# Order of the query products and one attention pipeline per layer in a three-layer transformer kernel

## The chip, the cores and the metric

The kernel runs on one core of a Trainium2 chip. The metric is the device time of one execution in microseconds (us). Everything is fp32. TensorE (PE) does matmuls and transposes, VectorE (DVE) and ScalarE (ACT) the elementwise work, SyncE (SP) issues the loads of the weights.

## The reference, cut to what matters

Three layers over 512 latent rows (x), the first two of them also with 256 context rows (c). Each layer has two attention branches, a and b, whose q, k and v are products of the same normalised input h:

```
p = h @ w_in[l]                          # 1024 wide; k, v, q of both branches, convolution, gates
ka, kb, qa, qb = rope(rmsnorm(head) * gain)   # per head of 64
o_a = softmax(qa ka' / 8) va             # layers 0, 1: all keys, latent and context
o_b = softmax(qb kb' / 8, sink) vb       # layers 0, 1: a window of 128 each way, and the context
o_c = short_conv(p)
x = x + gt1 * ((g_a*(o_a@w0) + g_b*(o_b@w1) + g_c*(o_c@w2)) @ w_out)
x = x + gt2 * expert_choice_ffn(...)     # layers 0 and 1 only
```

Layer 0 also computes the context rows' outputs. Layer 1 needs only keys and values of the context. Layer 2 has a branch a with a causal band and a branch b with a dilated causal pattern, gates of its own, and no experts.

## The kernel before, in words

Activations lie transposed, features on the partitions and rows along the free axis. A product of 128 output features takes 8 pairs of weight load and matmul for 512 columns, and in the layers with context columns 8 more for the 256; 128 features of weights are half of a 1 MB chunk, and the chunks come through a ring of six buffers that SP fills in the order of use (L1014): a chunk is loaded as soon as the last product of the chunk six before it is through.

The order of work is a list of jobs written out by hand for each layer (`plan_layer` L296, `plan_second` L314). Every engine goes through the same list and does its part of each job, in that order:

- `("qk", l, name)`: the product of a q or k (TensorE), its square into `sq` (ACT), the copy of the product into its buffer (DVE). The copy releases the PSUM slot.
- `("hs", ...)`: one matmul that sums the squares by head, the square root into `rs` (ACT), `reciprocal` (L1434) and the scaling (L1436) (DVE).
- `("rot", ...)`: one matmul that permutes for the rotation (L762), three DVE operations (L1440 to L1443).
- `("v", l, n)`: 96 matmuls of 128 columns (L727) and a copy by ACT.
- `pipelined` (L278) puts behind each job of a list the `rot` of the qk two before it and the `hs` of the qk before it.

A PSUM slot of two banks is taken for every product, `hs`, `rot` and `v`, three slots in turn (L629 `begin`), so in a row of qk jobs each product gets the slot of the product before it. ACT's square of a job waits until the `hs` before it has read `sq` (L1188), and the root of an `hs` waits until the rotation before it is through with `rs`.

Attention is worked on in units: one tile of 128 queries times a pair of heads. `attention_order` (L247) makes a software pipeline over the units of one branch, a step per unit s: S(s) are its scores (L773, into slots 0 and 1; the step waits for both), E(s) the masked copy with row maximum (DVE L1510) and the exponential (ACT L1132), T(s-1) the transposes (L785) and their copies, V the product with v for two units (L818), spread over two steps and three steps late; Q, K, R and O are the row sums and the scaled output of four units (one tile). A pipeline of n units has n+3 steps. Layer 0 has 24 units per branch (the last eight are context units with 2 tiles of keys), layers 1 and 2 have 16. Units of branch a have 6 tiles of keys in layers 0 and 1, units of b 4 or 5; in layer 2 they have 1 or 2 (a) and 1 to 4 (b).

Before, layers 0 and 1 go: ka, va, kb, vb, qa0 to qa3, the pipeline of branch a, qb0 to qb3, the pipeline of branch b, convolution, gates. Both branches' queries lie in the same buffer `qbuf` (`q3`), so qb can't be made ahead of the end of branch a. Layer 2 makes all k, q and v and its gates first (`plan_second`), and then goes through two pipelines one after the other.

```
            first = [("qk", l, "ka"), ("v", l, 0), ("qk", l, "kb"), ("v", l, 1)]
            first += [("qk", l, f"qa{j}") for j in range(4)]
...
            order = pipelined(first) + attention_order((l, 0))
            order += pipelined([("qk", l, f"qb{j}") for j in range(4)])
            order += attention_order((l, 1)) + conv + gates[2] + gates[0] + gates[1]
```

Of the kernel before, what the change touches and what calls it, by code (L numbers as in the profile page):

```python
# [101 lines left out]
def program(nc, x, c, ctx_in, c_ctx, w_ada, b_ada, g_mix, g_ffn, w_in, qg_a, kg_a, qg_b, kg_b, sink_b, conv_w,  # L102
            w_branch, w_out, w_router, w_e_gate, w_e_up, w_e_down, norm_gain_2, w_in_2, q_norm_a_2, k_norm_a_2,
            sinks_a_2, q_norm_b_2, k_norm_b_2, w_out_2, consts, out):
    with ExitStack() as stack:
# [104 lines left out]
        def units_first(l, br):  # L210
            units = []
            streams = [("x", i) for i in range(NX // P)] + ([("c", i) for i in range(NC // P)] if l == 0 else [])
            for st, i in streams:
                q0, mask = (i * P if st == "x" else NX + i * P), None
                if st == "c":
                    segs, lo, hi, tiles = [(0, NC, NX)], 0, NC, [4, 5]
                elif br == 0:
                    segs, lo, hi, tiles = [(0, NX, 0), (NX, NC, NX)], 0, NT, list(range(6))
                elif i == 0:
                    segs, lo, hi, tiles, mask = [(512, 2 * P, 0), (768, NC, NX)], 512, 1024, [0, 1, 4, 5], 3 * P  # L220
                else:
                    n = min(3, NX // P + 1 - i)
                    segs, lo, hi, mask = [(256, NC, NX), (512, n * P, (i - 1) * P)], 256, 512 + n * P, 0
                    tiles = [4, 5] + [i - 1 + m for m in range(n)]
                for g in range(4):
                    units.append(dict(q0=q0, t=q0 // P, g=g, heads=(g, 4 + g), kj=br,
                                      segs=segs, lo=lo, hi=hi, tiles=tiles, mask=mask, vcols=(0, HD)))
            return units

        def units_second(br):  # L230
            units = []
            for i in range(NX // P):
                a = max(0, i - 1) if br == 0 else 0
                n = (i - a + 1) * P
                for g in range(4):
                    heads = (g, 4 + g) if br == 0 else (2 * g, 2 * g + 1)
                    units.append(dict(q0=i * P, t=i, g=g, heads=heads, kj=0 if br == 0 else g, segs=[(0, n, a * P)],
                                      lo=0, hi=n, tiles=list(range(a, i + 1)),
                                      mask=M_BAND + 2 * P - n if br == 0 else M_DIL + 4 * P - n,
                                      vcols=(0, HD) if br == 0 else (P + heads[0] * HD, P + heads[1] * HD)))  # L240
# [6 lines left out]
        def attention_order(key):  # L247

            units = UNITS[key]
            n = len(units)  # L250
            order = []
            for s in range(n + 3):
                banks = (len(units[s - 1]["tiles"]) + 1) // 2 if 1 <= s <= n else 0
                if s < n:
                    order.append(("S", key, s))
                if s % 4 == 0 and 4 <= s <= n:
                    order.append(("Q", key, s // 4 - 1))
                if banks:
                    order.append(("T", key, s - 1, 0))
                if s < n:  # L260
                    order.append(("E", key, s))
                    if s % 4 == 3 and key in SINK:
                        order.append(("K", key, s // 4))
                if banks > 1:
                    order.append(("T", key, s - 1, 1))
                if s % 4 == 1 and s >= 5:
                    order.append(("R", key, s // 4 - 1))
                if s >= 3:
                    h, part = (s - 3) // 2, (s - 3) % 2
                    if h < n // 2:  # L270
                        order.append(("V", key, h, part))
                        if part and h % 2:
                            order.append(("O", key, h // 2))
                if banks > 2:
                    order.append(("T", key, s - 1, 2))
            return order
# [311 lines left out]
        def last_rot(key):  # L588
            return ("rot", key[0], "qb3" if key[1] else "qa3")
# [12 lines left out]
        def turned_to(j):  # L602

            key, p, b = j[1:]
            n = min(2, len(UNITS[key][p]["tiles"]) - 2 * b)
            to = turned[key[0] == 2][:, p // 2 % 2, 2 * b:2 * b + n, :, p % 2, :]
# [3 lines left out]
        def last_v(key):  # L610
            return ("v", key[0], 2 if key == (2, 1) else key[1])
# [6 lines left out]
        def _(pe):  # L618
# [76 lines left out]
            def run(j):  # L695
                kind, l = j[0], j[1]
                if kind in ("qk", "conv_c", "conv_x", "conv_b", "gate", "silg", "branch", "wout"):
# [4 lines left out]
                    if kind == "branch":  # L702
# [3 lines left out]
                        elif d == 0:  # L706
                            need(oT_ready, ("O", (l, br), len(UNITS[l, br]) // 4 - 1))
                        product(j, None, w, q3 if br == 2 else o4[:, br], wd, 4)
                    elif kind == "wout":
                        if j[2] == 0 and l < 2:  # L710
                            need(gate_used, ("branch", l, 1, KD - 1))
                        elif j[2] == 0:
                            need(oT_ready, ("O", (2, 0), NX // P - 1))
                            need(oT_ready, ("O", (2, 1), NX // P - 1))
# [49 lines left out]
                elif kind == "S":  # L764
                    u = UNITS[j[1]][j[2]]
                    q, k, _ = attn_bufs(j[1])
                    if j[2] == 0:
                        need(q_ready, last_rot(j[1]))
# [24 lines left out]
                elif kind == "V":  # L793
                    key, h, late = j[1:]
                    u = UNITS[key][2 * h]
                    v = attn_bufs(key)[2]
                    if h == 0 and not late:
                        need(v_ready, last_v(key))
                    n = o_number[key, h // 2]
                    if not late:  # L800
                        for r in range(2):
                            last = [t for t in bank_jobs[r] if t[0] == "T" and t[1] == key and t[2] // 2 == h]
# [5 lines left out]
                    exps = turned[key[0] == 2][:, h % 2]  # L808
                    tiles, own = u["tiles"], key == (2, 1)
                    steps = [(g, m, a) for g in (range(2) if own else (None,)) for m in range(len(tiles)) for a in range(2)]  # L810
                    cut = len(steps) // 4 * 2 or 1
                    for g, m, a in steps[cut:] if late else steps[:cut]:
                        r = slice(a * HD, (a + 1) * HD)
                        if own:
                            out_, exp_, col = ps[r, b + g * P:b + (g + 1) * P], exps[:, m, a, g, :], UNITS[key][2 * h + g]["vcols"][a]
# [311 lines left out]
        def _(act):  # L1127
# [46 lines left out]
            def run(j):  # L1174
# [64 lines left out]
                elif kind == "R" and j[1][0] < 2:  # L1239
# [118 lines left out]
        def _(dve):  # L1358
# [63 lines left out]
            def run(j):  # L1422
                kind, l = j[0], j[1]
                w = width(l, j[2] if kind in ("qk", "hs") else "") if kind not in ("S", "E", "K", "Q", "T", "R", "V", "O") else 0
# [71 lines left out]
                elif kind == "S":  # L1496
# [5 lines left out]
                    for a in range(2):  # L1502
# [6 lines left out]
                        least = nsink[:, SINK[j[1]], h:h + 1] if j[1] in SINK else 3.0e38  # L1509
# [3 lines left out]
                    if j[2] % 4 == 3 and j[1] in SINK:  # L1513
                        sink = by_pair(sinks[:, SINK[j[1]], :])
                        V.do(v.tensor_tensor(sinkd[:, t % 2, :].rearrange("p (g a) -> p g a", a=2), sink,
                                             nms[:, t % 2, :].rearrange("p (g a) -> p g a", a=2), ALU.add), sd_ready, ("K", j[1], t))
                elif kind == "Q":
                    key, t = j[1:]
                    V.need(p_ready, ("E", key, 4 * t + 3, 1))
                    if key in SINK:  # L1520
                        V.need(sx_ready, ("K", key, t))
                        V.do(v.tensor_tensor(lsum[:, t % 2, :], lsum[:, t % 2, :], sinke[:, t % 2, :], ALU.add))
                    V.do(v.reciprocal(rden[:, :], lsum[:, t % 2, :]))
                    if t > 0:
                        V.need(tb_full[bank_of["R", key, t - 1]], ("R", key, t - 1))
# [8 lines left out]
                elif kind == "R" and j[1][0] == 2:  # L1534
                    r = bank_of[j]
                    sg = sg2[:, 4 * j[1][1]:4 * j[1][1] + 4, j[2] * P:(j[2] + 1) * P]
# [3 lines left out]
                elif kind == "O":  # L1540
                    (l, br), t = j[1:]
                    V.need(pv_done, ("V", j[1], 2 * t + 1, 1))
# [3 lines left out]
                    if l < 2:  # L1546
                        V.need(tb_done[bank_of["R", j[1], t]], ("R", j[1], t))
# [155 lines left out]
```

How the kernel before makes its waits and increments, by code:

```python
            def meet():  # L623
                phases[0] += 1
                pe.sem_inc(s_phase, 1)
                pe.wait_ge(s_phase, 4 * phases[0])
# [1 line left out]
            def begin(key, slot=None):  # L629
                if slot is None:
                    slot, turn[0] = turn[0], (turn[0] + 1) % 3
                if slot == 2 and in_banks[0]:
                    for r in range(2):
                        pe.wait_ge(tb_done[r].sem, bank_at[r])
                    in_banks[0] = False
                n = used[slot]
                used[slot] += 1
                job[key] = [slot, n, None]
                if n:
                    pe.wait_ge(free[slot], n)
                return BANK[slot]
# [8 lines left out]
            def begin_bank(j):  # L651
                r = bank_of[j]
                if not in_banks[0]:
                    pe.wait_ge(free[2], used[2])
                    in_banks[0] = True
                if bank_at[r]:
                    pe.wait_ge(tb_done[r].sem, bank_at[r])
                bank_at[r] += 1
                return TBANK[r]
# [1 line left out]
            def weights(key):  # L662
                n = chunk_key[key]
                slot, value = chunk_at[n]
                pe.wait_ge(w_full[slot], value)
                return n, slot
# [1 line left out]
            def need(ev, key):  # L669
                pe.wait_ge(ev.sem, ev.at[key])
# [24 lines left out]
            def run(j):  # L695
# [36 lines left out]
                    if j == FIRST[0]:
                        pe.wait_ge(sil_ready, 1)
                    b = begin(j)
```

## Time and profile before

| | us |
|---|---|
| median of 3 runs | 3743.57 (3741.46 to 3747.7) |
| the profiled execution | 3751.16 |
| its span, first to last instruction | 3749.4 |
| TensorE busy | 3290.6 (88%) |
| VectorE busy | 886.3 (24%) |
| ScalarE busy | 622.7 (17%) |
| TensorE clock granted, mean | 0.951 |

The span is one execution, and all rows below are from it. TensorE's end times are modelled, so a matmul's busy time runs some 0.16 us into the next group; where a duration matters it is read from start to start. "Idle before" in a timeline is the time in which the engine had nothing to do ahead of a group, and the arrow names what ended it. "DVEq L1117" is VectorE's release of a PSUM slot.

### The profile page before, as it was taken

Reading aid. Unit: us, or ns where it says so; the run is one execution under the profiler, and the core shown is the slowest. Engines: PE = TensorE matmul, PEld = TensorE weight load, DVE = VectorE, ACT = ScalarE, POOL = GpSimd, SP = SyncE. Lnnn points to the kernel's source line nnn. Section 1 sums busy time; section 2 is a strip of 40 time slices with the busy share of each in tenths; the row PEclk is TensorE's granted clock in tenths of the full one; section 3 lists DMA queues with packets and bytes.
Section 4 is the critical chain, followed back from the end, with each engine's and each line's share of the span. In section 5 each row is a group of like instructions: output and inputs, shape, how many; then the busy total and the mean of one; then the engine's idle time right before and its main releaser. Section 6 shows DMA issues by size and latency. Waiting matters only on the chain. (4 is left out here: it accounts for less than half of the span.)

```text
span 3749.4 us, 36326 instructions
## 1 busy us (share of the span) xinstructions
PE 3290.6 (88%) x14258; PEld 1628.0 (43%) x14258; DVE 886.3 (24%) x1357; ACT 622.7 (17%) x1072; POOL 16.8 (0%) x35
## 2 busy tenths in 40 slices
PE   5887899989995999999987979999778788778978
PEld 3544555545554442433344544444423223233544
DVE  2464611001114001111024562011300010025342
ACT  2162600000002100101021541000201001011141
POOL 1000000000000000000000000000000000000000
PEclk8989999999996999999988989999799999999989
DMA  7100012353510778697851001232188998961200
GB/s 205 45 1 23 1 45 79 124 174 106 169 56 12 262 277 313 238 347 255 313 151 45 1 23 57 58 88 79 34 317 298 356 329 312 358 200 45 68 1 23
DMA packets 381924, 551.94 MB, mean 147 GB/s; under 512 B 65496, under 2 KB 177384, under 8 KB 381640
## 3 DMA queue, kind: packets, MB, share of 16 engines
q1 hardware_dynamic: 379856, 546.53, 42.8%
q0 software_dynamic: 1600, 3.20, 0.3%
q8 instruction: 107, 1.75, 0.2%
q14 instruction: 49, 0.40, 0.0%
q10 hardware_dynamic: 312, 0.05, 0.0%
HBM read 547.63 MB, written 2.10 MB: 147 GB/s over the span
## 5 line engine op out<-in xcount | busy, mean ns | idle before, releaser
L692 PE MATMUL ps<-hT,ring 128*128 128x512 f32 (+1 forms) x2576 | 973.9, 536 | 72.8 <-ACT hT L1132 28.4
L899 PE MATMUL ps<-ring,hT 128*64 128x512 f32 x3072 | 716.8, 604 | 112.3 <-DMA ring<-in_w_e_up 41.2
L692 PEld LDWEIGHTS ps<-hT,ring 128*128 128x128 f32 x2576 | 492.5, 192 | 545.1 <-issue 492.1
L899 PEld LDWEIGHTS ps<-ring,hT 128*64 128x64 f32 x3072 | 202.0, 137 | 604.4 <-issue 401.7
L692 PE MATMUL ps<-obuf,ring 128*128 128x512 f32 (+1 forms) x512 | 198.5, 540 | 2.5 <-DMA ring<-in_w_branch 1.5
L1659 DVE SCALAR_TENSOR_TENSOR xT<-ps,mod,xT 128x512 f32<-128x512 f32 x96 | 63.5, 662 | 535.1 <-PE ps L967 281.1
L905 PE MATMUL ps<-ring,hT 128*32 128x512 f32 x1536 | 184.7, 598 | 0.0
L1132 ACT ACTIVATE prob<-prob,nms 128x768 f32<-128x768 f32 (+5 forms) x224 | 159.2, 711 | 59.9 <-DVE nms L1510 51.8
L1132 ACT ACTIVATE prob<-ps 128x512 f32<-128x512 f32 (+1 forms) x56 | 38.6, 689 | 733.0 <-PE ps L692 733.0
L862 PE MATMUL ps<-obuf,merged 128*128 128x256 f32 x640 | 153.3, 389 | 7.3 <-DVE obuf L1611 4.1
L785 PE MATMUL ps<-con,prob 128*128 128x128 f32 x872 | 135.8, 291 | 26.4 <-ACT prob L1132 25.2
L773 PE MATMUL ps<-kbuf,qbuf 64*128 64x256 f32 (+3 forms) x640 | 124.2, 502 | 26.4 <-DVEq L1117 16.7
L1434 DVE RECIPROCAL rs<-rs 128x512 f32<-128x512 f32 (+1 forms) x33 | 129.9, 3935 | 72.8 <-ACT rs L1132 72.4
L692 PE MATMUL ps<-merged,ring 128*128 128x512 f32 (+1 forms) x384 | 139.7, 526 | 4.1 <-issue 4.1
L692 PEld LDWEIGHTS ps<-obuf,ring 128*128 128x128 f32 x512 | 96.2, 190 | 99.4 <-issue 93.8
L785 PEld LDWEIGHTS ps<-con,prob 128*128 128x128 f32 x872 | 96.8, 146 | 92.3 <-ACT prob L1132 52.0
L862 PEld LDWEIGHTS ps<-obuf,merged 128*128 128x128 f32 x640 | 119.9, 195 | 35.2 <-issue 20.7
L963 PE MATMUL ps<-kbuf,obuf 128*128 128x512 f32 x256 | 115.7, 592 | 0.0
L1475 DVE TENSOR_TENSOR prob<-prob,ps 128x768 f32<-128x768 f32 (+1 forms) x32 | 26.3, 822 | 358.0 <-PE ps L692 358.0
L1643 DVE TENSOR_TENSOR qbuf<-qbuf,ps 128x1536 f32<-128x1536 f32 (+1 forms) x16 | 23.8, 1488 | 340.8 <-ACT qbuf L1132 340.8
L692 PEld LDWEIGHTS ps<-merged,ring 128*128 128x128 f32 x384 | 73.4, 192 | 70.4 <-issue 67.1
L1645 DVE TENSOR_TENSOR qbuf<-qbuf,ps 128x1536 f32<-128x1536 f32 (+1 forms) x16 | 23.8, 1488 | 317.4 <-PE ps L905 162.4
(185 smaller groups left out, 2292.3 us busy)
## 6 DMA issues: line engine op xcount, KB each, us to landing
ring<-in_w_e_gate SPq DMA_DIRECT2D x256, 512.0 KB, 7.4
ring<-in_w_e_up SPq DMA_DIRECT2D x256, 512.0 KB, 8.2
ring<-in_w_e_down SPq DMA_DIRECT2D x256, 512.0 KB, 7.8
ring<-in_w_in SPq DMA_DIRECT2D x49, 1024.0 KB, 5.2
ring<-in_w_ada SPq DMA_DIRECT2D x48, 1024.0 KB, 11.6
ring<-in_w_in SPq DMA_DIRECT2D x48, 256.0 KB, 5.0
ring<-in_w_branch SPq DMA_DIRECT2D x16, 512.0 KB, 7.3
ring<-in_w_out SPq DMA_DIRECT2D x8, 1024.0 KB, 8.6
```

The source lines that it names most:

```text
L692: mm = pe.matmul(ps[:, b + a:b + e], lhs[:, k, :], rhs[:, k, a:e], start=k == 0, stop=k == nk - 1)
L773: mm = pe.matmul(ps[:, b[a] + c0:b[a] + c0 + w], q[r, u["g"], u["q0"]:u["q0"] + P], k[r, u["kj"], k0:k0 + w], start=True, stop=True)
L785: mm = pe.transpose(ps[:, o:o + P], scored(j[2], a, u)[:, m * P:(m + 1) * P], ident)
L862: mm = pe.matmul(ps[:, o:o + 2 * P], tok[:, t, d * P:(d + 1) * P], selx[:, t, :], start=t == 0, stop=t == 3)
L899: mm = pe.matmul(ps[e * CX:(e + 1) * CX, b + pair * 512:b + (pair + 1) * 512], lhs[:, k, s0:s0 + CX], expert_dst(slot, e)[:, k % 2, :], st ...
L905: mm = pe.matmul(ps[e * CC:(e + 1) * CC, b + 1024:b + 1536], lhs[:, k, s0:s0 + CC], expert_dst(slots[e // 2], e % 2)[:, k % 2, :], start=k ...
L963: mm = pe.matmul(ps[:, o:o + NX], ye[:, g, d * P:(d + 1) * P], gTx[:, g, :], start=g == 0, stop=g == 1)
L1132: return sc.activation(o, i, f, **kw)
L1434: V.do(v.reciprocal(rs[:, 0:w], rs[:, 0:w]))
L1475: V.do(v.tensor_tensor(g, g, ps[:, b:b + w], ALU.mult))
L1643: step(v.tensor_tensor(g, g, banks(("eg", half)), ALU.mult))
L1659: step(v.scalar_tensor_tensor(xT[:, d, a:e], ps[:, o:o + e - a], mod3[:, l, GT2 + d, a // 512:a // 512 + 1], xT[:, d, a:e], ALU.mult, ALU. ...
```

## The change

In layers 0 and 1 the queries of branch a and b go into `obuf` (`o4`), each into the place where its branch's output will lie: scores of tile t read queries of tile t, and the output of tile t is written after them. So all eight query products come before attention. The two v products are moved from behind ka and kb to the end of the list. In all three layers the units of both branches form one list and one pipeline (48+3 steps in layer 0, 32+3 in layers 1 and 2, in the place of two times 24+3 and 16+3). Waits that a branch's first unit had (rotated queries, values ready) are kept for the first unit of each branch. Job names lose the branch; `Q`, `O`, `R` and `K` are numbered through both branches. No arithmetic, no load and no matmul is added or taken away.

```
-        UNITS = {(l, br): units_first(l, br) for l in range(DEPTH) for br in range(2)}
-        UNITS |= {(2, br): units_second(br) for br in range(2)}
+        UNITS = {l: units_first(l, 0) + units_first(l, 1) for l in range(DEPTH)}
+        UNITS[2] = units_second(0) + units_second(1)
+        TILES = {l: len(UNITS[l]) // 8 for l in UNITS}
...
         def plan_layer(l):
-            first = [("qk", l, "ka"), ("v", l, 0), ("qk", l, "kb"), ("v", l, 1)]
-            first += [("qk", l, f"qa{j}") for j in range(4)]
+            first = [("qk", l, "ka"), ("qk", l, "kb")] + [("qk", l, f"{w}{j}") for w in ("qa", "qb") for j in range(4)]
+            first += [("v", l, 0), ("v", l, 1)]
...
-            order = pipelined(first) + attention_order((l, 0))
-            order += pipelined([("qk", l, f"qb{j}") for j in range(4)])
-            order += attention_order((l, 1)) + conv + gates[2] + gates[0] + gates[1]
+            order = pipelined(first) + attention_order(l) + conv + gates[2] + gates[0] + gates[1]
...
-            return (pipelined(first) + attention_order((2, 0)) + attention_order((2, 1))
-                    + [("wout", 2, d) for d in range(KD)])
+            return pipelined(first) + attention_order(2) + [("wout", 2, d) for d in range(KD)]
...
         def qk_dest(l, name):
             if l < 2:
-                return {"ka": k3[:, 0, :], "kb": k3[:, 1, :]}.get(name) if name[0] == "k" else q3[:, int(name[2]), :]
+                return {"ka": k3[:, 0, :], "kb": k3[:, 1, :]}.get(name) if name[0] == "k" else o4[:, "ab".index(name[1]), int(name[2]), :]
...
-        def attn_bufs(key):
-            l, br = key
+        def attn_bufs(l, br):
             if l < 2:
-                return q3, k3, lambda t, c0: v4[:, br, t, c0:c0 + HD]
+                return o4[:, br], k3, lambda t, c0: v4[:, br, t, c0:c0 + HD]
...
+        def first_of_branch(l, p):
+            return p % (len(UNITS[l]) // 2) == 0
...
                 elif kind == "S":
-                    if j[2] == 0:
-                        need(q_ready, last_rot(j[1]))
+                    if first_of_branch(l, j[2]):
+                        need(q_ready, last_rot(l, u["br"]))
...
                 elif kind == "V":
-                    if h == 0 and not late:
-                        need(v_ready, last_v(key))
+                    if first_of_branch(l, 2 * h) and not late:
+                        need(v_ready, last_v(l, u["br"]))
```

## Rows read from the trace of the kernel before

**Rows 1.** The page: busy time and share of the span by engine.
```profile
PE 3290.6 (88%) x14258; PEld 1628.0 (43%) x14258; DVE 886.3 (24%) x1357; ACT 622.7 (17%) x1072; POOL 16.8 (0%) x35
```
**Rows 2.** Stretches: us, busy PE, PEld, DVE, ACT, POOL, then clock, DMA share, GB/s.
```profile
87.16:200.54 113.38, 90.04 (x390) 59.24 (x388) 54.03 (x36) 13.15 (x15) 0.00 (x0) 0.91 0.11 38
303.60:381.01 77.41, 54.08 (x154) 29.54 (x152) 36.71 (x25) 9.41 (x10) 0.00 (x0) 0.84 0.09 27
1965.47:2059.36 93.89, 74.61 (x317) 45.10 (x315) 45.50 (x36) 11.44 (x15) 0.00 (x0) 0.91 0.14 45
2143.89:2201.61 57.72, 38.66 (x82) 15.40 (x80) 28.18 (x25) 7.71 (x10) 0.00 (x0) 0.84 0.11 37
```
**Rows 3.** Timeline of TensorE, layer 0, ahead of branch a's attention.
```profile
99.17 10.48 PE L692 MATMUL ps<-hT,ring 128*128 128x512 f32 x32
109.49 1.02 PE L762 MATMUL ps<-kbuf,con 128*128 128x512 f32 x2
110.35 10.88 PE L727 MATMUL ps<-ring,hT 128*128 128x128 f32 x96
...
145.14 10.48 PE L692 MATMUL ps<-hT,ring 128*128 128x512 f32 x32
...
156.32 1.45 PE L756 MATMUL ps<-sq,con 128*128 128x512 f32 x4
159.98 10.56 PE L692 MATMUL ps<-hT,ring 128*128 128x512 f32 x32 [2.21 <-DVEq L1117]
...
184.24 2.08 PE L762 MATMUL ps<-qbuf,con 128*128 128x512 f32 x2 [11.56 <-DVE qbuf L1436]
...
196.04 2.08 PE L762 MATMUL ps<-qbuf,con 128*128 128x512 f32 x2 [7.16 <-DVE qbuf L1436]
200.54 2.93 PE L773 MATMUL ps<-kbuf,qbuf 64*128 64x512 f32 x8 [2.42 <-DVE qbuf L1443]
```
**Rows 4.** Timeline of ScalarE, layer 0, ahead of branch a's attention.
```profile
189.98 1.28 ACT L1132 ACT_TABLE_LOAD   x1
```
**Rows 5.** Stretches: DMA behind layer 0's first product; layer 2's row of qk jobs.
```profile
76.00:97.00 21.00, 20.20 (x119) 15.25 (x118) 5.74 (x9) 6.87 (x11) 0.00 (x0) 0.98 0.00 0
...
3394.00:3494.00 100.00, 81.84 (x181) 32.72 (x180) 62.15 (x55) 12.16 (x19) 0.00 (x0) 1.00 0.20 48
```
**Rows 6.** Timeline of TensorE, layer 2, two of its qk jobs.
```profile
3406.75 7.11 PE L692 MATMUL ps<-hT,ring 128*128 128x512 f32 x16 [1.73 <-DVEq L1117]
3414.02 1.13 PE L762 MATMUL ps<-qbuf,con 128*128 128x512 f32 x2 [0.17 <-DVE qbuf L1436]
...
3417.73 7.11 PE L692 MATMUL ps<-hT,ring 128*128 128x512 f32 x16 [1.73 <-DVEq L1117]
```
**Rows 7.** Timeline of VectorE, layer 2, in one of these jobs.
```profile
3409.83 3.35 DVE L1434 RECIPROCAL rs<-rs 128x512 f32<-128x512 f32 x1 [0.88 <-ACT rs L1132]
```
**Rows 8.** Stretches: ends and beginnings of the attention pipelines, columns as in rows 2.
```profile
299.40:303.60 4.20, 2.75 (x22) 1.52 (x20) 0.63 (x2) 2.47 (x7) 0.00 (x0) 1.00 0.00 0
381.01:393.24 12.23, 9.12 (x40) 6.20 (x41) 5.30 (x14) 5.20 (x12) 0.00 (x0) 0.59 0.00 0
393.24:471.88 78.64, 71.48 (x497) 42.82 (x497) 49.28 (x128) 54.03 (x129) 0.00 (x0) 0.96 0.01 1
2136.70:2143.89 7.19, 6.45 (x53) 4.10 (x52) 1.48 (x4) 2.72 (x6) 0.00 (x0) 1.00 0.01 2
2201.61:2213.20 11.59, 8.52 (x40) 5.88 (x41) 5.30 (x14) 4.96 (x11) 0.00 (x0) 0.62 0.00 0
3624.70:3634.00 9.30, 5.11 (x36) 2.88 (x37) 3.97 (x17) 4.51 (x17) 0.00 (x0) 0.98 0.00 0
```
**Rows 9.** Timeline of VectorE, first scores of branch a in layer 0.
```profile
208.87 0.96 DVE L1510 CUSTOM_DVE_ANT_0 prob<-ps,zero 128x768 f32<-128x768 f32 x1 [3.14 <-PE ps L773]
...
212.97 0.96 DVE L1510 CUSTOM_DVE_ANT_0 prob<-ps,zero 128x768 f32<-128x768 f32 x1 [1.14 <-PE ps L773]
```
**Rows 10.** Stretches of low or full clock, columns as in rows 2.
```profile
216.00:288.00 72.00, 70.88 (x506) 42.88 (x503) 42.90 (x91) 51.13 (x101) 0.00 (x0) 1.00 0.00 1
...
3582.00:3598.00 16.00, 11.92 (x44) 6.16 (x42) 6.39 (x29) 9.46 (x30) 0.00 (x0) 0.51 0.01 2
```

More of the change, by code:

```diff
@@ L225, in units_first @@
                 for g in range(4):
-                    units.append(dict(q0=q0, t=q0 // P, g=g, heads=(g, 4 + g), kj=br,
+                    units.append(dict(br=br, q0=q0, t=q0 // P, g=g, heads=(g, 4 + g), kj=br,
                                       segs=segs, lo=lo, hi=hi, tiles=tiles, mask=mask, vcols=(0, HD)))
@@ L236, in units_second @@
                     heads = (g, 4 + g) if br == 0 else (2 * g, 2 * g + 1)
-                    units.append(dict(q0=i * P, t=i, g=g, heads=heads, kj=0 if br == 0 else g, segs=[(0, n, a * P)],
+                    units.append(dict(br=br, q0=i * P, t=i, g=g, heads=heads, kj=0 if br == 0 else g, segs=[(0, n, a * P)],
                                       lo=0, hi=n, tiles=list(range(a, i + 1)),
@@ L254, in attention_order @@
                 if s < n:
-                    order.append(("S", key, s))
+                    order.append(("S", l, s))
                 if s % 4 == 0 and 4 <= s <= n:
-                    order.append(("Q", key, s // 4 - 1))
+                    order.append(("Q", l, s // 4 - 1))
                 if banks:
-                    order.append(("T", key, s - 1, 0))
+                    order.append(("T", l, s - 1, 0))
                 if s < n:
-                    order.append(("E", key, s))
-                    if s % 4 == 3 and key in SINK:
-                        order.append(("K", key, s // 4))
+                    order.append(("E", l, s))
+                    if s % 4 == 3 and (l, units[s]["br"]) in SINK:
+                        order.append(("K", l, s // 4))
                 if banks > 1:
-                    order.append(("T", key, s - 1, 1))
+                    order.append(("T", l, s - 1, 1))
                 if s % 4 == 1 and s >= 5:
-                    order.append(("R", key, s // 4 - 1))
+                    order.append(("R", l, s // 4 - 1))
                 if s >= 3:
@@ L270, in attention_order @@
                     if h < n // 2:
-                        order.append(("V", key, h, part))
+                        order.append(("V", l, h, part))
                         if part and h % 2:
-                            order.append(("O", key, h // 2))
+                            order.append(("O", l, h // 2))
                 if banks > 2:
-                    order.append(("T", key, s - 1, 2))
+                    order.append(("T", l, s - 1, 2))
             return order
@@ L586, in program, with last_rot @@
         PARAM_DMAS = (3 + 1 + 8 + 1 + 2, 3 + 1 + 8 + 1 + 1 + 8 + 1)
-        def last_rot(key):
-            return ("rot", key[0], "qb3" if key[1] else "qa3")
+        def last_rot(l, br):
+            return ("rot", l, "qb3" if br else "qa3")
         def scored(p, a, u):
@@ L602, in turned_to, with last_v @@
         def turned_to(j):
-            key, p, b = j[1:]
-            n = min(2, len(UNITS[key][p]["tiles"]) - 2 * b)
-            to = turned[key[0] == 2][:, p // 2 % 2, 2 * b:2 * b + n, :, p % 2, :]
+            l, p, b = j[1:]
+            n = min(2, len(UNITS[l][p]["tiles"]) - 2 * b)
+            to = turned[l == 2][:, p // 2 % 2, 2 * b:2 * b + n, :, p % 2, :]
             at = TBANK[bank_of[j]]
             return to, ps[:, at:at + n * 256].rearrange("p (k a t) -> p k a t", k=n, a=2)
-        def last_v(key):
-            return ("v", key[0], 2 if key == (2, 1) else key[1])
+        def last_v(l, br):
+            return ("v", l, 2 if (l, br) == (2, 1) else br)
+        def first_of_branch(l, p):
+            return p % (len(UNITS[l]) // 2) == 0
         o_number = {j[1:]: n for n, j in enumerate(of("O"))}
@@ L793, in run @@
                 elif kind == "V":
-                    key, h, late = j[1:]
-                    u = UNITS[key][2 * h]
-                    v = attn_bufs(key)[2]
-                    if h == 0 and not late:
-                        need(v_ready, last_v(key))
-                    n = o_number[key, h // 2]
+                    h, late = j[2:]
+                    u = UNITS[l][2 * h]
+                    v = attn_bufs(l, u["br"])[2]
+                    if first_of_branch(l, 2 * h) and not late:
+                        need(v_ready, last_v(l, u["br"]))
+                    n = o_number[l, h // 2]
                     if not late:
                         for r in range(2):
-                            last = [t for t in bank_jobs[r] if t[0] == "T" and t[1] == key and t[2] // 2 == h]
+                            last = [t for t in bank_jobs[r] if t[0] == "T" and t[1] == l and t[2] // 2 == h]
                             if last:
@@ L1238, in run @@
                     A.do(sc.copy(*turned_to(j)), tb_done[r], j)
-                elif kind == "R" and j[1][0] < 2:
+                elif kind == "R" and l < 2:
                     r = bank_of[j]
@@ L1423, in run @@
                 kind, l = j[0], j[1]
-                w = width(l, j[2] if kind in ("qk", "hs") else "") if kind not in ("S", "E", "K", "Q", "T", "R", "V", "O") else 0
+                w = width(l, j[2] if kind in ("qk", "hs") else "")
                 if kind == "adat":
@@ L1508, in run @@
                         h = u["heads"][a]
-                        least = nsink[:, SINK[j[1]], h:h + 1] if j[1] in SINK else 3.0e38
+                        least = nsink[:, SINK[l, u["br"]], h:h + 1] if (l, u["br"]) in SINK else 3.0e38
                         V.do(v.tensor_tensor_reduce(scored(j[2], a, u), ps[:, b + u["lo"]:b + u["hi"]], mask, -SCALE, least,
@@ L1512, in run @@
                         V.release(j + (a,))
-                    if j[2] % 4 == 3 and j[1] in SINK:
-                        sink = by_pair(sinks[:, SINK[j[1]], :])
+                    if j[2] % 4 == 3 and (l, u["br"]) in SINK:
+                        sink = by_pair(sinks[:, SINK[l, u["br"]], :])
                         V.do(v.tensor_tensor(sinkd[:, t % 2, :].rearrange("p (g a) -> p g a", a=2), sink,
@@ L1533, in run @@
                     V.do(v.tensor_copy(*turned_to(j)), tb_done[r], j)
-                elif kind == "R" and j[1][0] == 2:
+                elif kind == "R" and l == 2:
                     r = bank_of[j]
-                    sg = sg2[:, 4 * j[1][1]:4 * j[1][1] + 4, j[2] * P:(j[2] + 1) * P]
+                    br, t = divmod(j[2], TILES[2])
+                    sg = sg2[:, 4 * br:4 * br + 4, t * P:(t + 1) * P]
                     V.need(tb_full[r], j)
```

35 lines of the change are left out of this document (17 added, 18 removed).

## The prediction

> **What bounds the kernel now.** The page first: TensorE is busy 88% of the span, nothing else over 24% [rows 1], so what can be won without less work are the 12% in which TensorE idles or runs at the low clock. The stretches by stage come next, since the change touches only a few. In layers 0 and 1 the products ahead of branch a's attention take 113.4 and 93.9 us, the qb products ahead of branch b's 77.4 and 57.7; TensorE is busy 90.0, 74.6, 54.1 and 38.7 us of that, at a mean clock of 0.84 to 0.91 [rows 2]. The timeline shows where the holes are: not among the first products, where a v product (10.9 us) covers the chain of the job before, but behind the last one. There hs, square root, reciprocal, scaling and rotation of two jobs run out with nothing beside them: idle 11.6, 7.2 and 2.4 us, and what is left of TensorE's work runs at 1.2 GHz (the rotation takes 2.08 us in the place of 1.02) [rows 3]. This tail of some 28 us comes four times, twice in each of the layers 0 and 1. The engines beside are no bound there: VectorE is busy in half of each stretch at most [rows 2].
>
> **The sum, layer 0.** Durations from start to start [rows 3]: a product 10.32, rot 0.86, hs 1.45 less the overlap of 0.16, so 1.29, v 10.72 us. Where qk jobs follow each other, each product waits for the slot of the one before (its square and copy): a gap of some 2.4 us, and a period of 159.98 - 145.14 = 14.84 us. Before, this gap comes once in each of the two stretches, since v products or first jobs fill the other places. After, from the end of the first product: kb, hs, qa0, rot, hs = 24.1; seven periods (qa1 to qb3) = 103.9; then gap 2.4, v, rot, hs, v, rot = 26.8; and about 1.0 until the rotation's slot is free for the first scores. Together 155.8 us. The chain of the last query (root, reciprocal 5, scaling 1, some 8 us in all) fits behind the last v product of 10.7. Before it is 113.4 + 77.4 = 190.8 [rows 2]. Gain 35.0 us: four idle tails less, six or so gaps more.
>
> **Layer 1.** Queries are 512 wide, a product is 6.87 us. The nearest rows are layer 2's, whose jobs already follow each other so, 512 wide: period 3417.73 - 3406.75 = 10.98 us, with 1.7 us ahead of the product and 0.2 ahead of the rotation, which waits for VectorE's scaling [rows 6]. The period is the chain's: square, copy, three operations of the rotation, root, reciprocal 3.35, scaling, rot, hs [rows 7]. After, from the end of ka's product: kb 10.3, hs 1.3, qa0 6.9, a wait of about 1.4 for ka's scaling, rot 0.9, hs 1.3 = 22.0; one period lengthened by kb's 768 columns to about 13.0; six of 10.98 = 65.9; 1.9 to the start of v; v, rot, hs, v, rot and the slot = 25.0. Together 127.8 against 93.9 + 57.7 = 151.6 [rows 2]. Gain 23.8 us.
>
> **Where the branches join.** Three steps of running out and three of filling become three steps that do both. Layer 0: 4.2 + 12.2 us before; a step of branch b takes (78.6 - 4.2)/21 = 3.5 us on average, three 10.6 [rows 8]. Gain 5.8. Layer 1: 7.2 + 11.6 before. TensorE's work in it is 6.5 us and 8.5 at a clock of 0.62, so about 5.3 at full clock: 11.8, and with a wait or two 12.3 [rows 8]. Gain 6.5. Layer 2: 9.3 us with 5.1 of work [rows 8]; its steps wait for the exponentials anyway, so I take about half of the idle time: 2.0, between 0 and 4.2.
>
> **The first scores.** They start at 1.2 GHz now. VectorE waits 3.14 us for the scores of such a step and 1.14 at full clock [rows 9]; the two first steps of each layer could be some 1.4 us shorter, 2.8 for a layer, 5.6 for both. This asks that the clock stays up while the pipeline fills. Against it: in layer 2 the fill begins behind dense products and the clock is at 0.51, all but 1.2 GHz, through 16 us of it [rows 10]; its units are smaller than these. For it: the row of gapped jobs in layer 2 [rows 5] and steady attention [rows 10] hold 1.00. I take one of the two: 2.8, between 0 and 5.6; it can't be a loss, since these steps run at the low clock already.
>
> **What costs nothing, and its cover.** The DMAs: both k and v products use the same chunk, so the kv chunks are held until the v products at the end. All six chunks up to qb fit into the ring of six, and behind layer 0's first product there is no traffic any more [rows 5], so they have landed. What comes later is SP's load of the first two convolution chunks, which now waits for v0 and v1; the cover is the whole of attention. Were it gone, six chunks of 1 MB would come one by one. Position of the v products: their first reader is V three steps into attention, behind both copies. Queries in `obuf`: same size and engine, no operation more. In-order engines: ACT's copy of v1 stands ahead of the first exponential only, VectorE's last rotation ahead of the first row maximum; both are in the 1.0 us above. The gaps grow from one of 2.4 us per stretch to seven in a row: cover for the clock is that layer 2's ten such jobs ran at 1.00 [rows 5]. ACT's tables: one switch to the square root and one back less in each of the two layers. The load takes 1.28 us and ends 4.8 us before the rotation that TensorE waits for [rows 3, 4], while VectorE's reciprocal runs, so I count 0. "ScalarE: Activation LUTs" of the Trainium skill (section "What ACT_TABLE_LOAD costs") asks 2.66 us for every switch, drain included, and by it the sum would be up to 10.6 us larger; the trace agrees with its load time but shows it off the path here.
>
> **Sum.** 35.0 + 23.8 + 5.8 + 6.5 + 2.0 + 2.8 = 75.9 us. Against the profiled execution's 3751.2 us this gives 3675.3; that execution is 7.6 us above the median of the runs, so for the median 3743.6 - 75.9 = **3667.7, say 3668 us**.
>
> **Rivals.**
> (1) *The joined pipeline brings nothing.* The steps at the join could be as long as the old ones together, as each then holds S of branch b, T and V of a, and waits for the ACT chain; and the fill falls to the low clock. Then only the products' gain stays: 58.8, 3685 us. For it: layer 2's steps wait for ACT. Against: in layers 0 and 1 TensorE is busy in most of such steps. Chance 0.12.
> (2) *More than counted.* The fills keep the clock (2.8 more), layer 2's join gives all 4.2, and of layer 0's end, where the last steps now are as before, nothing. 3663, and with a join in layers 0 and 1 that is bounded by TensorE alone (2 to 3 us more each) 3657. Chance 0.15.
> (3) *The other side: the low clock in the gapped rows.* Place: the seven periods of qk jobs in layers 0 and 1. Price: at 1.2 GHz the 12.5 us of TensorE's work in a period of layer 0 and some 8.6 in layer 1 double: 7 x 12.5 + 7 x 8.6 = 148 us. Then 3668 + 148 = 3816, slower by 72. It decides from the point where over half of these periods run at the low clock (75.9 of 148 us). For it: the clock did fall to 1.2 GHz in the tails, with holes of 7 to 12 us [rows 2, 3]. Against it: 100 us of layer 2 with holes of 1.7 us every 11 and a clock of 1.00 [rows 5, 6]; layer 0's holes of 2.2 are longer but come at every 15 us. Chance 0.03.
> (4) *The chain of the products moves only.* If something that isn't in the trace serialises v and the last queries (a slot, `sq`), each layer keeps one tail half: 12 us less gain in each, 3692. In the slot order, products and v share one slot, rot and hs have the other two, and I find no such wait. Chance 0.04. That the change doesn't do what it says, no change of time, is about 0.01: the lists are plain.
>
> **How the numbers follow.** The forecast has 0.65, rivals 0.12, 0.15, 0.03, 0.04 and 0.01. Unknown costs around the forecast are the fills (0 to 5.6), the joins (layer 2 0 to 4.2; 2 each elsewhere), and 3 us to each side for the spread of the runs; with 3657 of rival 2 and most of 3685 of rival 1 this is 3654 to 3684. A measurement of this kernel can tell 0.2% (some 7.5 us) from no change. All but rival 3 and the last are faster by far more: 0.96 faster, 0.01 within, 0.03 slower.
>
> **What would show it.** In the profile after: from the end of layer 0's first product to the first scores some 156 us, layer 1's 128; gaps ahead of products named "DVEq" of 2.2 us seven times in layer 0, plus one ahead of v0, and of 1.7 in layer 1 with a clock of 1.00; no wait of 7 or 11 us of a rotation for the scaling. VectorE's and ScalarE's busy time all but unchanged, ScalarE with four table loads less. At the join no clock below 1.00 in layers 0 and 1. The forecast is wrong if a clock of 0.5 stands in the rows of products, if a wait for the ring shows at the first convolution product, or if the stretch from branch a's first scores to b's last output isn't shorter by 5 to 9 us in layers 0 and 1.

## The result and the profile after

The changed kernel takes 3681.5 us at the median of four runs (3676.2 to 3682.7), against 3745.3 for the kernel before: 64 us less, a ratio of 0.9828 with a 95% interval of 0.9812 to 0.9843. The forecast was 3668, the range 3654 to 3684. Every time in this document is from fast executions; one of the four with longer gaps in layer 1 took 7863 us and is left out.

The profiled execution of after has a span of 3680.9 us, 68.5 below the one of before. Before's profiled execution lies 5.9 us above its median and after's 1.1, which is the difference to the 64. From the page of after, the busy times and the costliest group of matmuls, and then the same group before:

```profile
PE 3271.4 (89%) x14258; PEld 1618.8 (44%) x14258; DVE 886.2 (24%) x1357; ACT 617.0 (17%) x1068; POOL 16.7 (0%) x35
...
L692 PE MATMUL ps<-hT,ring 128*128 128x512 f32 (+1 forms) x2576 | 982.1, 540 | 94.0 <-DVEq L1116 43.0
```

```profile
L692 PE MATMUL ps<-hT,ring 128*128 128x512 f32 (+1 forms) x2576 | 973.9, 536 | 72.8 <-ACT hT L1132 28.4
```

VectorE's work is what it was [rows 1], ScalarE has four instructions less, the table loads, TensorE 19 us less: the same matmuls, fewer of them at the low clock. But the products from `hT`, which should all be as fast as before, have more busy time, not less (before 973.9 us, now 982.1), and 43 us of idle time ahead of them that end with VectorE's release of a slot. The gaps were foreseen, the longer busy time was not.

The stretches of after, in the columns of [rows 2]: attention of the three layers, then the products of layers 0 and 1, from the end of ka's product to the first scores.

```profile
252.40:437.83 185.43, 168.72 (x1168) 101.11 (x1168) 112.75 (x273) 128.97 (x283) 0.00 (x0) 0.98 0.09 29
2061.18:2205.60 144.42, 135.74 (x960) 83.53 (x960) 92.03 (x193) 97.66 (x197) 0.00 (x0) 0.99 0.12 37
3518.56:3611.67 93.11, 72.56 (x513) 42.11 (x513) 52.57 (x176) 58.45 (x165) 0.00 (x0) 0.91 0.00 1
85.77:252.40 166.63, 147.99 (x542) 91.33 (x540) 88.74 (x59) 19.63 (x23) 0.00 (x0) 0.94 0.02 7
1932.93:2061.18 128.25, 108.93 (x397) 58.72 (x396) 71.62 (x59) 16.17 (x23) 0.00 (x0) 1.00 0.03 9
```

And attention of before, which the rows ahead of the prediction show only in parts:

```profile
200.54:303.60 103.06, 94.50 (x632) 55.55 (x632) 56.13 (x129) 69.52 (x142) 0.00 (x0) 0.95 0.00 1
381.01:471.88 90.87, 80.60 (x537) 49.02 (x537) 54.59 (x141) 59.23 (x140) 0.00 (x0) 0.91 0.01 1
2059.36:2143.89 84.53, 79.39 (x528) 47.74 (x528) 46.57 (x91) 54.03 (x100) 0.00 (x0) 0.93 0.00 1
2201.61:2269.44 67.83, 61.99 (x433) 39.31 (x433) 43.41 (x99) 43.33 (x96) 0.00 (x0) 0.94 0.00 1
3581.60:3680.21 98.61, 76.72 (x513) 43.98 (x513) 52.52 (x176) 58.51 (x165) 0.00 (x0) 0.86 0.01 1
```

| stretch | before | after | gain | forecast |
|---|---|---|---|---|
| products, layer 0 | 190.8 | 166.6 | 24.2 | 35.0 |
| products, layer 1 | 151.6 | 128.3 | 23.4 | 23.8 |
| attention, layer 0 | 193.9 | 185.4 | 8.5 | 5.8 and a fill |
| attention, layer 1 | 152.4 | 144.4 | 7.9 | 6.5 and a fill |
| attention, layer 2 | 98.6 | 93.1 | 5.5 | 2.0 |
| all the rest | | | -1.0 | 0 |

The fills were forecast at 2.8 us in all. So one term fell short by 10.8 us, layer 0's products, and the attention terms gave 4.8 more than their 17.1. The timeline of TensorE in layer 0 shows the first at once:

```profile
97.38 10.48 PE L692 MATMUL ps<-hT,ring 128*128 128x512 f32 x32
...
112.21 12.26 PE L692 MATMUL ps<-hT,ring 128*128 128x512 f32 x32 [2.20 <-DVEq L1116]
...
128.82 12.25 PE L692 MATMUL ps<-hT,ring 128*128 128x512 f32 x32 [2.21 <-DVEq L1116]
...
145.43 12.26 PE L692 MATMUL ps<-hT,ring 128*128 128x512 f32 x32 [2.21 <-DVEq L1116]
...
162.04 10.56 PE L692 MATMUL ps<-hT,ring 128*128 128x512 f32 x32 [2.21 <-DVEq L1116]
...
176.95 12.26 PE L692 MATMUL ps<-hT,ring 128*128 128x512 f32 x32 [2.21 <-DVEq L1116]
...
225.08 12.58 PE L726 MATMUL ps<-ring,hT 128*128 128x128 f32 x96 [2.21 <-DVEq L1116]
...
252.40 1.56 PE L772 MATMUL ps<-kbuf,obuf 64*128 64x512 f32 x8 [1.00 <-DVEq L1116]
256.40 2.93 PE L772 MATMUL ps<-kbuf,obuf 64*128 64x512 f32 x8 [2.44 <-DVEq L1116]
```

The gaps are there as forecast, eight of 2.2 us. But six of the eight jobs behind them take 1.7 us more than the same job elsewhere: the products at 112, 129, 145, 177 and 194 us, and the first v product at 225. The clock by stretches of 2 us around the first gap, and around the one at 162 us that has no such effect:

```profile
110.00:112.00 2.00, 0.01 (x1) 0.00 (x0) 0.95 (x1) 0.81 (x1) 0.00 (x0) 1.00 0.00 0
112.00:114.00 2.00, 1.79 (x3) 0.97 (x4) 1.67 (x4) 0.00 (x0) 0.00 (x0) 0.68 0.03 8
114.00:116.00 2.00, 2.00 (x3) 0.68 (x2) 0.91 (x2) 0.90 (x1) 0.00 (x0) 0.50 0.00 0
116.00:118.00 2.00, 2.00 (x6) 0.91 (x5) 2.00 (x1) 0.00 (x0) 0.00 (x0) 0.97 0.00 0
...
162.00:164.00 2.00, 1.96 (x5) 1.04 (x6) 1.82 (x3) 0.00 (x0) 0.00 (x0) 1.00 0.00 0
164.00:166.00 2.00, 2.00 (x6) 0.81 (x6) 0.91 (x2) 0.90 (x1) 0.00 (x0) 1.00 0.04 8
```

TensorE idles 2.2 us, starts again at full clock, and is then at 1.2 GHz for some 3.4 us (what 0.68, 0.50 and 0.97 come to in three slices of 2 us). Six times 1.7 are 10.2 of the missing 10.8 us. Layer 1, with gaps of 1.7 us, shows none of this: clock 1.00 through its whole row of jobs, and a gain within 0.4 us of the sum.

### The profile page after: what moved, and what is told of

It is laid out like the page before. It is cut to its first block and busy times, and to the rows that moved or that the text cites. A ratio compares the mean times of both kernels' runs of the same rounds, so it can differ in the third digit from the quotient of the medians.

```text
span 3680.9 us, 36321 instructions
## 1 busy us (share of the span) xinstructions
PE 3271.4 (89%) x14258; PEld 1618.8 (44%) x14258; DVE 886.2 (24%) x1357; ACT 617.0 (17%) x1068; POOL 16.7 (0%) x35
## 5 line engine op out<-in xcount | busy, mean ns | idle before, releaser
L692 PE MATMUL ps<-hT,ring 128*128 128x512 f32 (+1 forms) x2576 | 982.1, 540 | 94.0 <-DVEq L1116 43.0
L692 PEld LDWEIGHTS ps<-obuf,ring 128*128 128x128 f32 x512 | 96.2, 190 | 98.6 <-issue 94.1
L772 PE MATMUL ps<-kbuf,obuf 64*128 64x256 f32 (+2 forms) x576 | 103.6, 473 | 11.1 <-DVEq L1116 10.0
L1643 DVE TENSOR_TENSOR qbuf<-qbuf,ps 128x1536 f32<-128x1536 f32 (+1 forms) x16 | 23.8, 1488 | 342.1 <-ACT qbuf L1131 342.1
L1645 DVE TENSOR_TENSOR qbuf<-qbuf,ps 128x1536 f32<-128x1536 f32 (+1 forms) x16 | 23.8, 1488 | 316.0 <-PE ps L904 162.4
## 6 DMA issues: line engine op xcount, KB each, us to landing
ring<-in_w_ada SPq DMA_DIRECT2D x48, 1024.0 KB, 11.6
```

Source lines behind the costliest of these rows:

```text
L692: mm = pe.matmul(ps[:, b + a:b + e], lhs[:, k, :], rhs[:, k, a:e], start=k == 0, stop=k == nk - 1)
L772: mm = pe.matmul(ps[:, b[a] + c0:b[a] + c0 + w], q[r, u["g"], u["q0"]:u["q0"] + P], k[r, u["kj"], k0:k0 + w], start=True, stop=True)
L1643: step(v.tensor_tensor(g, g, banks(("eg", half)), ALU.mult))
```

## The experiments

The theory was: the change is worth what its idle tails were, less the gaps that it adds; the gaps are waits for a PSUM slot; and in layer 0 they are just long enough to bring the clock down. Eight runs tell its parts apart. All ratios are to the kernel before, timed in the same rounds.

| kernel | median, us | ratio (95% interval) |
|---|---|---|
| changed kernel again | 3679.2 | 0.9828 (0.9811 to 0.9844) |
| join undone | 3691.0 | 0.9856 (0.9840 to 0.9871) |
| v behind k again | 3699.4 | 0.9882 (0.9866 to 0.9899) |
| before, v last only | 3727.1 | 0.9942 (0.9925 to 0.9959) |
| rotation in banks of its own | 3660.0 | 0.9773 (0.9757 to 0.9789) |
| the same, head sum first | 3600.2 | 0.9615 (0.9600 to 0.9630) |
| longer gaps in layer 1 | 3694.0 | 0.9866 (0.9846 to 0.9886) |
| before, without gaps | 3691.9 | 0.9860 (0.9843 to 0.9876) |

**The join undone.** Two pipelines per layer again, all else as changed.

```
-            order = pipelined(first) + attention_order(l) + conv + ...
+            order = pipelined(first) + attention_order(l, 0) + attention_order(l, 1) + conv + ...
```

> The changed kernel with the join undone: all queries first and v last as in the change, but each layer goes through two attention pipelines, one per branch, again. Theory: the join is worth three steps per layer, 5.8 + 6.5 + 2.0 us by the prediction; but branch b's pipeline now fills right behind branch a's, with TensorE just busy, so some 3 us of low clock in layers 0 and 1 should stay away: 3692 us, between 3687 and 3701. Rival: the attention stretches are bounded by the steps' exponentials and the join brought nothing; the 8.5 and 7.9 us by which they are shorter in the profile after come from the clock alone: 3682 to 3684.

Measured 3691.0, 9.4 us above the changed kernel's 3681.5, as forecast. The attention stretches of this kernel:

```profile
253.22:439.08 185.86, 165.68 (x1168) 99.97 (x1168) 112.70 (x273) 128.95 (x283) 0.00 (x0) 1.00 0.09 29
2058.51:2208.33 149.82, 137.18 (x961) 84.95 (x961) 92.03 (x193) 97.66 (x197) 0.00 (x0) 0.98 0.11 35
3522.29:3620.00 97.71, 75.46 (x513) 43.53 (x513) 52.49 (x176) 58.45 (x165) 0.00 (x0) 0.88 0.00 1
```

Against after, the join is worth 0.4 us in layer 0, 5.4 in layer 1 and 4.6 in layer 2, 10.4 in all. The other 11.5 us of attention's gain are there without it: 8.1, 2.5 and 0.9, most of it in layer 0, where the clock is now 1.00 and was 0.95 and 0.91. The 0.9 is layer 2's, whose order of work is that of the kernel before again, so it shows what two executions can differ by.

The 0.4 of layer 0 is understated. In after the second step's scores take 2.93 us at the low clock (256.40 above), here 1.56; and in after the last steps of branch b run at the low clock too, here they don't. The same 20 matmuls, in after and then with the join undone:

```profile
433.60:437.83 4.23, 4.23 (x20) 2.27 (x20) 0.80 (x3) 1.31 (x3) 0.00 (x0) 0.60 0.00 0
```

```profile
436.28:439.08 2.80, 2.80 (x20) 1.49 (x20) 0.80 (x3) 1.31 (x3) 0.00 (x0) 1.00 0.00 0
```

Each of the two is worth 1.4 us, so the join's steps in layer 0 save some 3.2 us, of which 2.8 went to the low clock. Attention at full clock, with the tails gone, is worth more than the join there.

**The v products put back behind k.**

```
+            first = [("qk", l, "ka"), ("v", l, 0), ("qk", l, "kb"), ("v", l, 1)]
+            first += [("qk", l, f"{w}{j}") for w in ("qa", "qb") for j in range(4)]
```

> The changed kernel with only the v products put back behind ka and kb; queries of both branches first, joined pipeline. Theory: the tail of the last query (about 28 us in layer 0, 24 in layer 1) stands open again once per layer, and three gaps ahead of products per layer go: net about +17 us in layer 0 and +13 in layer 1, 3711 us. Rival: what covers the tail is not v but the longer row of queries itself, and the place of v is worth nothing: 3682.

Measured 3699.4, 18 us above the changed kernel. The tail is back, whole, once per layer; TensorE in layer 0:

```profile
247.44 2.07 PE L761 MATMUL ps<-obuf,con 128*128 128x512 f32 x2 [11.56 <-DVE obuf L1435]
...
259.23 2.07 PE L761 MATMUL ps<-obuf,con 128*128 128x512 f32 x2 [7.16 <-DVE obuf L1435]
262.31 2.93 PE L772 MATMUL ps<-kbuf,obuf 64*128 64x512 f32 x8 [1.00 <-DVEq L1116]
```

The place of v is worth 18 us, not 30: I had charged the whole 28 us of the tail, but what v covers is 11.6 + 7.2 of waiting and 3.5 of low clock, 22 us; and v's place adds three gaps in layer 0 and, by the count of slow jobs (three here, six in after), three falls of the clock: 6.6 + 5.1 us. In the stretches of products this kernel is 10.1 us longer than after in layer 0 (176.7 against 166.6) and 8.1 in layer 1 (136.3 against 128.3).

**Only v moved, in the kernel before.**

```
+            first = [("qk", l, "ka"), ("qk", l, "kb")] + [("qk", l, f"qa{j}") for j in range(4)]
+            first += [("v", l, 0), ("v", l, 1)]
```

> The kernel before with one part of the change: v products behind qa3 instead of behind ka and kb; qb still made between two pipelines. Theory: branch a's tail is covered in each layer (25 and 21 us of idle time less, 3 of low clock each), against three gaps more per layer (7 us and up to 5 of clock in layer 0, 7 in layer 1): about 26 us less than before, 3719 us. Rival: the tail only moves behind v: no change, 3745.

Measured 3727.1, 19 us below before; the mechanism holds and the size is again some two thirds of what I gave it. TensorE shows the same gaps, and the same low clock behind three of four of them ahead of branch a's attention in layer 0 (at 113, 130 and 161 us, not at 147):

```profile
113.32 12.26 PE L692 MATMUL ps<-hT,ring 128*128 128x512 f32 x32 [2.20 <-DVEq L1117]
...
129.93 12.26 PE L692 MATMUL ps<-hT,ring 128*128 128x512 f32 x32 [2.20 <-DVEq L1117]
...
146.53 10.56 PE L692 MATMUL ps<-hT,ring 128*128 128x512 f32 x32 [2.20 <-DVEq L1117]
...
161.45 12.58 PE L727 MATMUL ps<-ring,hT 128*128 128x128 f32 x96 [2.21 <-DVEq L1117]
```

Here queries go to `qbuf`, so where they are written isn't what slows the jobs.

**The gaps taken away.** The rotation's matmul writes to the two PSUM banks that only V uses, and `pipelined` issues each head sum ahead of the rotation of the job before. V's first products wait for these banks, and a root waits for the scaling of the job before, since it writes the same `rs`.

```
-                    b = begin(j)
+                    b = begin(j, 3 + rot_turn[0])
+                    rot_turn[0] = 1 - rot_turn[0]
...
-                if rots:
-                    order.append(rots.pop(0))
+                ready = rots.pop(0) if rots else None
                 if sums:
                     t = sums.pop(0)
                     order.append(("hs",) + t)
                     rots.append(("rot",) + t)
+                if ready:
+                    order.append(ready)
```

> The changed kernel with the cause of the gaps taken away: the rotation's matmul writes to the two PSUM banks that only V uses, so products and head sums have the three slots to themselves, and each head sum is issued ahead of the rotation of the job before it. Theory: the gaps (2.2 us in layer 0, 1.7 and 0.2 in layers 1 and 2) are waits for a slot, and the 12.25 us products of layer 0 are products whose start ran at the low clock after such a gap. So all products of layer 0 take 10.3 us, the period there is 12.5 us, in layers 1 and 2 about 8.7, the clock stays at 1.00: 29 us less in layer 0, 22 in layer 1, 25 in layer 2, about 3606 us. Rival: layer 0's products are slow for another reason than a gap (where they write, what VectorE does beside them): then they still take 12.25 us in most jobs, 3616. Rival: VectorE's chain of root, reciprocal, scaling and rotation bounds the period at 10.98 and 14 us anyway: about 3670.

Measured 3600.2, 81 us below the changed kernel and 145 below before. TensorE's timeline in layer 0:

```profile
109.26 10.48 PE L694 MATMUL ps<-hT,ring 128*128 128x512 f32 x32
...
121.73 10.48 PE L694 MATMUL ps<-hT,ring 128*128 128x512 f32 x32
```

The whole stretch of layer 0's products, columns as in [rows 2]:

```profile
84.57:221.26 136.69, 136.57 (x544) 87.93 (x543) 87.97 (x58) 18.76 (x23) 0.00 (x0) 1.00 0.03 8
```

A period of 12.47 us (121.73 - 109.26), TensorE busy all the time, clock 1.00, no slow product. Layer 0's stretch is 30 us shorter than after's 166.6 (29 expected). Both rivals are out: without the gap no product is slow, and VectorE keeps up once the head sum doesn't queue behind a rotation.

**Shorter gaps.** Only the banks, not the order.

> The changed kernel with the rotation's matmul in PSUM banks of its own but the order of head sum and rotation left alone, so that products wait for no slot, while the chain square, copy, rotation, root, reciprocal, scaling, rotation, head sum stays closed. Theory: in layers 1 and 2 the period is that chain's and stays near 11.0 us, the 1.7 us only move from the product to the rotation; in layer 0 the chain takes about 14.1 us against 14.8, and the gap shrinks from 2.2 to some 1.6 us ahead of the rotation. If a gap of 1.6 us leaves the clock alone, layer 0 gains 10 us of slow products and 5 + 2 of gaps, layers 1 and 2 some 2 to 5 us together: 3662 us. Rival: the length of a gap isn't what matters, and the clock falls here too: 3672.

Measured 3660.0. The product waits no more, the rotation does; layer 0:

```profile
121.99 1.12 PE L763 MATMUL ps<-kbuf,con 128*128 128x512 f32 x2 [1.23 <-DVE kbuf L1439]
...
124.24 10.48 PE L693 MATMUL ps<-hT,ring 128*128 128x512 f32 x32
...
135.96 1.12 PE L763 MATMUL ps<-obuf,con 128*128 128x512 f32 x2 [1.24 <-DVE obuf L1439]
...
208.08 10.88 PE L727 MATMUL ps<-ring,hT 128*128 128x128 f32 x96
```

Gaps of 1.24 us, and every product at full clock. In layer 1 the gap before the rotation is 2.13 us in most periods, where after has 1.7 and 0.2 apart, and there the clock is no longer 1.00 throughout (0.95; two of the products take 7.7 and 7.8 us in the place of 7.0). One of the two:

```profile
1989.71 1.24 PE L763 MATMUL ps<-obuf,con 128*128 128x512 f32 x2 [2.13 <-DVE obuf L1439]
...
1992.45 7.81 PE L693 MATMUL ps<-hT,ring 128*128 128x512 f32 x16
```

Layer 2 shows the same behind three of seven gaps of 2.13 us. The two waits of a period, put together, are worse than apart. Of the 81 us of the run before, the banks alone give 21; the other 60 need the order, with the shorter wait of the root.

**Longer gaps.** In layer 1 VectorE copies each query twice.

```
+                    if l == 1 and j[2][0] == "q":
+                        V.do(v.tensor_copy(qk_dest(*j[1:])[:, 0:w], ps[:, b:b + w]))
```

> The changed kernel with the copy of each query product in layer 1 made twice, which lengthens that layer's gaps from 1.7 to about 2.5 us and nothing else. Theory: a gap's length decides on the clock, so layer 1, which held 1.00 through its row of jobs, now shows slow product starts as layer 0 does: 5.8 us for the copies and up to 8 times 1.7 for the clock, 3681 + 6 + 10 = 3697 us. Rival: the clock falls in layer 0 for another reason (its wider jobs), layer 1 stays at 1.00: 3687.

Measured 3694.0 (3685.2, 3694.0 and 3694.6), 12.5 us above the changed kernel (16 expected), where the copies alone are 6. The profile is of the first, the shortest of the three; layer 1's stretch of products in it is 12.5 us longer too, 140.72 against the 128.25 of after, so the cost stands where it was put:

```profile
1925.34:2066.06 140.72, 116.25 (x397) 63.05 (x396) 77.14 (x67) 16.17 (x23) 0.00 (x0) 0.94 0.03 9
```

TensorE in layer 1, which had 7.1 us for every product:

```profile
1963.96 7.10 PE L692 MATMUL ps<-hT,ring 128*128 128x512 f32 x16 [2.45 <-DVEq L1116]
...
1975.66 8.78 PE L692 MATMUL ps<-hT,ring 128*128 128x512 f32 x16 [2.45 <-DVEq L1116]
...
2001.57 8.80 PE L692 MATMUL ps<-hT,ring 128*128 128x512 f32 x16 [2.45 <-DVEq L1116]
...
2014.54 7.11 PE L692 MATMUL ps<-hT,ring 128*128 128x512 f32 x16 [2.45 <-DVEq L1116]
```

Five of its eight gaps now have a job behind them that takes 1.7 us longer. That is the same price as in layer 0, brought about in another layer by 0.7 us more of idle time: the wider jobs aren't needed for it, a longer gap is enough. It doesn't decide alone, since three of the eight are spared, the first two among them.

**The changed kernel again.**

> The changed kernel once more, beside the three that follow. Theory: the gaps of 2.2 us in layer 0 are at the edge of what brings the clock down, so how many of the eight are followed by a slow product differs from run to run while the gaps stay 2.2 us (six of eight in the profile after): 3681 us, 4 us to each side. Rival: the fall belongs to certain jobs, and the same six places show it again.

Measured 3679.2. The gaps of layer 0 are 2.2 us again, and the same six places are followed by a slow job, so the rival was nearer: which gaps count is largely the same from run to run. In the kernel with the join undone, whose layer 0 has the same order up to attention, it was the seventh and not the eighth, the other five the same. Why the fourth is spared each time stays open.

**The kernel before without gaps.**

> The kernel before with the gaps taken out in the same way as in the run with own banks and head sum first. It has only two such gaps in layer 0, two in layer 1 and eleven in layer 2. Theory: 5 us less in layer 0, 5 in layer 1, 26 in layer 2: 3709 us; the change itself is then worth 3709 - 3600 = 109 us in place of 64, the difference being the gaps that the change adds and the slow clock behind them. Rival: without gaps the change is worth the same as with them, 64 us: 3664.

Measured 3691.9, 52 us below before and not 36. The change is worth 92 us without gaps (3691.9 to 3600.2), against 64 with them and 109 expected. What I had missed stands in its timeline of layer 0: with the head sum issued first, the last but one rotation waits 7.35 us, not 11.56.

```profile
176.37 2.07 PE L765 MATMUL ps<-qbuf,con 128*128 128x512 f32 x2 [7.35 <-DVE qbuf L1442]
178.24 2.77 PE L758 MATMUL ps<-sq,con 128*128 128x512 f32 x4
188.17 2.07 PE L765 MATMUL ps<-qbuf,con 128*128 128x512 f32 x2 [7.17 <-DVE qbuf L1442]
```

In before, the root of that job waited for VectorE's rotation of the job ahead of it (head sum at 171.23 us, root at 177.17); here the root starts right behind its head sum (166.71 and 169.10). The two tails of layer 0 are 4.2 us shorter by this, those of layer 1 3.6 and 3.9 (waits of 5.0 + 6.1 and 5.0 + 5.8 in the place of 9.0 + 5.7), some 16 in all, which the change can then no longer win. The rival's 3664 is out.

## Why the prediction was right, and where it was off

**What bounds it.** The tails were the cost. Their waits of 11.6 and 7.2 us are gone in after and return with v put back, and v's place alone takes 19 us off the kernel before.

**Layer 0's products, 35.0 forecast, 24.2 found.** The step that failed is the sentence that the cover for the clock is layer 2's ten jobs at 1.00. Those gaps are 1.7 us; layer 0's are 2.2. The prediction saw the difference, and set against it that they come at every 15 us. Its last paragraph calls the forecast wrong if a clock of 0.5 stands in the rows of products, and one does (0.50 at 114 to 116 us). (The sum speaks of four idle tails in layer 0; they are two, with two long waits each, and the 35.0 is worked out rightly. Without the six slow jobs the stretch would be 156.4 us, against 155.8.) Rival 3 had the mechanism right, the place right for layer 0 and not for layer 1, and the price wrong: the clock doesn't stay down for a period, it costs 1.7 us per gap, 10.2 in all. By itself that could not have turned the sign: eight such gaps in each of two layers would cost 27 us against a gain of 76.

**Layer 1's products, 23.8 forecast, 23.4 found.** The period of 10.98 taken from layer 2, and the longer first one, were exact (gaps of 1.7 and 0.2, clock 1.00).

**Joins and fills, 14.3 and 2.8 forecast, 10.4 and 11.5 found.** The sum was 4.8 us too low, the split was off by more, so that the sum came near is luck: by layer the joins gave 0.4, 5.4 and 4.6 where 5.8, 6.5 and 2.0 were forecast. I charged branch b's slow fill to the join, and it goes by the tail's removal, with or without one pipeline. In layer 0 the join's steps save some 3.2 us, and the low clock at attention's second step and at its end took 2.8 of them back. Why it is 3.2 and not 5.8 stays open; the steps of the context units ahead of the join wait 0.4 to 0.8 us for ScalarE's exponential in both kernels, and no run takes that wait away. At the joins of layers 0 and 1 the clock is 1.00, as forecast.

**At no cost.** The tables: ScalarE has four loads less, and layer 1's stretch agrees within 0.4 us with a sum that counted them at 0, and layer 0's within 0.6 once the slow jobs are taken off. So of the 10.6 us estimated from the Trainium skill's "ScalarE: Activation LUTs" (section "What ACT_TABLE_LOAD costs") nothing can be seen: off the path, these loads cost nothing that shows. The held chunks: no wait for the ring at the end of attention in after. The rival of no gain at the join is out by the run with the join undone. The one of a tail half kept (12 us less in each layer) is out by layer 1's 23.4, and in layer 0, which did miss 10.8, by the timeline: no rotation waits there at all.

**The size as a whole.** 75.9 forecast, 64 measured, and 68.5 between the two profiled executions: 10.8 and 0.4 missing at the products, 4.8 more at attention, 1.0 lost elsewhere. The measured time is within the range thanks to rival 1's side of it, for another reason than rival 1 gave, and that is luck.

## What to carry to other kernels

A row of small dependent jobs should be priced by its gaps twice: the idle time, and the work behind each gap if the gap is long enough to touch the clock; take the gap's length and the clock behind it from rows with the same gap, not from like-looking ones with a shorter gap. And before moving work to cover a tail, look at what makes the gaps: here a slot order and the place of one small matmul in the queue were worth 81 us on top of the change's 64, and change and repair are worth more together than the one and the other apart (145 us, against 64 and 52).

## What was not expected of the hardware

In these rows of dense products an idle time of about 2 us is already followed by the low clock, in some places and not in others. Behind gaps of 1.24 us (layer 0, rotation in banks of its own) and 1.7 us (layers 1 and 2 in every kernel that has them) no job was slow. Behind gaps of 2.13 us five of eleven were, behind the 2.2 us of layer 0 six of eight in after and 31 of 44 in all traces together, behind 2.45 us five of eight. In before neither of the two gaps of 2.2 us in layer 0 was; with only v moved, the one ahead of branch b's attention was (a product of 12.25 us). So the length isn't all of it, and what else decides stays open: a wait of 2.25 us ahead of kb's rotation in layer 1 is not followed by the low clock in after, one of 2.24 us is in the kernel before with only v moved. Each time TensorE was at 1.2 GHz for some 3.4 us, and the work behind the gap took 1.7 us longer. The clock of a long stretch barely shows this (0.9 in the page's tenths, 0.94 over the stretch); a group of matmuls that takes 12.26 us where its neighbour takes 10.56 does.
